# Two output projections with the low activation beside the high one in 512-column matmuls, and both halves of the bank added by VectorE

## What is computed

```python
def even_layer(h, w_in, conv_w, conv_b, gx_w, gx_b, ga_w, ga_b, lru_lambda, sinks, w_out):
    ...
    return jnp.concatenate([y_a, y_b], axis=-1) @ w_out

def odd_layer(h, w_in, q_norm, w_uq, kv_norm, w_ukv, lambda_q1, lambda_k1, lambda_q2, lambda_k2,
              subln, w_out):
    ...
    return jnp.concatenate([y_c, y_d], axis=-1) @ w_out

def second_block(...):
    for layer in range(DEPTH_2):
        h = rmsnorm_2(x, norm_gains[layer])
        if layer % 2 == 0:
            x = x + even_layer(h, *even_params)
        else:
            x = x + odd_layer(h, *odd_params)
    return rmsnorm_2(x, final_norm_gain)
```

## Time and profile before

| | |
|---|---|
| median of 3 runs | 2313.37 us (2312.64 to 2315.13) |
| the profiled execution's own time | 2312.69 us |
| its span | 2310.9 us |
| granted TensorE clock, mean | 0.987 of full |
| TensorE matmul busy | 2070.4 us, 90% |
| VectorE busy | 1248.6 us, 54% |
| ScalarE busy | 868.1 us, 38% |

### The profile page before, as it was taken

How to read it: one execution, slowest core, us unless ns; L and a number is a source line. 1 busy time by engine, 2 the same in 40 slices (tenths; PEclk the granted TensorE clock), 3 DMA queues, 4 the chain that set the end, 5 groups by cost and what they waited for, 6 DMA issues and landing times.

```text
span 2310.9 us, 38449 instructions
## 1 busy us (share of the span) xinstructions
PE 2070.4 (90%) x14546; PEld 1350.6 (58%) x14546; DVE 1248.6 (54%) x2271; ACT 868.1 (38%) x1329; POOL 55.0 (2%) x56
## 2 busy tenths in 40 slices
PE   6899998998988888888888888899999999999998
PEld 2677767772222222222222222799899999998898
DVE  3455567545444444444444444677766554468655
ACT  3343344431211111111111111567756544466654
POOL 0000000000000000000000000110100000011000
PEclk9999999999999999999999999899999999999999
DMA  9998876889999999999999999554445555543443
GB/s 373 366 350 302 311 285 243 293 337 404 427 427 428 427 428 427 428 427 427 428 428 427 427 427 427 198 175 147 141 146 183 176 177 185 178 157 119 142 126 112
DMA packets 121943, 695.42 MB, mean 301 GB/s; under 512 B 13536, under 2 KB 13664, under 8 KB 60384
## 3 DMA queue, kind: packets, MB, share of 16 engines
q1 hardware_dynamic: 121824, 693.78, 77.8%
HBM read 691.63 MB, written 2.10 MB: 300 GB/s over the span
## 4 chain that ended last, share of the span: by engine, by line
PE 45%; DMA 34%; DVE 10%; ACT 5%; SPq 3%; issue 3%; DVEq 0%; ACTq 0%
DMA ring<-in_w 30%; PE acc L1289 29%; DVE WL L2045 3%; PE psO L1348 3%; DMA land<-in_stream_a 3%; PE psS L1557 3%; PE acc L1286 3%; ACT WH L1726 2%; SPq L1103 2%; DMA land<-in_stream_bc 1%; PE acc L1156 1%; PE psM L1156 1%; PE psO L1228 1%; DVE HL L2058 1%; DVE X L2200 1%
## 5 line engine op out<-in xcount | busy, mean ns | idle before, releaser
L2045 DVE TENSOR_TENSOR WL<-land,WH 128x1024 fp32r<-128x1024 f32 (+2 forms) x346 | 416.9, 1206 | 396.1 <-ACT WH L1726 391.8
L1289 PE MATMUL acc<-HH,WH 128*128 128x256 f32 x2000 | 586.2, 293 | 4.2 <-DVE HL L2064 2.2
L1289 PE MATMUL acc<-HH,WL 128*128 128x256 f32 x2000 | 568.9, 284 | 0.0
L1289 PE MATMUL acc<-HL,WH 128*128 128x256 f32 x2000 | 568.5, 284 | 0.0
L1726 ACT ACTIVATE WH<-land 128x1024 fp32r<-128x1024 f32 (+2 forms) x350 | 362.5, 1037 | 207.7 <-PE acc L1289 151.8
L1289 PEld LDWEIGHTS acc<-HH,WH 128*128 128x128 f32 x2000 | 386.8, 193 | 26.5 <-issue 12.6
L1289 PEld LDWEIGHTS acc<-HH,WL 128*128 128x128 f32 x2000 | 387.1, 194 | 2.6 <-issue 2.0
L1289 PEld LDWEIGHTS acc<-HL,WH 128*128 128x128 f32 x2000 | 386.5, 193 | 0.0
L1557 PE MATMUL psS<-ring,low 128*32 128x512 f32 x2048 | 272.6, 604 | 102.3 <-DMA ring<-in_w 100.6
L1557 PEld LDWEIGHTS psS<-ring,low 128*32 128x32 f32 x2048 | 40.7, 108 | 312.7 <-DMA ring<-in_w 284.8
L1887 ACT ACT_TABLE_LOAD x32 | 41.1, 1283 | 442.1 <-PE psS L1557 442.1
(11 more groups left out here) (425 smaller groups left out, 2611.7 us busy)
## 6 DMA issues: line engine op xcount, KB each, us to landing
ring<-in_w SPq DMA_DIRECT2D x384, 1024.0 KB, 26.0
land<-in_stream_bc SPq DMA_DIRECT2D x246, 512.0 KB, 4.1
land<-in_stream_a SPq DMA_DIRECT2D x92, 1024.0 KB, 8.0
land<-in_stream_a SPq DMA_DIRECT2D x100, 512.0 KB, 6.6
land<-in_stream_bc SPq DMA_DIRECT2D x12, 384.0 KB, 3.7
X<-in_xT SPq DMA_DIRECT2D x1, 2048.0 KB, 15.7
out<-low SPq DMA_DIRECT2D x3, 512.0 KB, 2.7
cst<-in_const SPq DMA_DIRECT2D x1, 1514.5 KB, 10.4
```

What stands on the lines that cost most here:

```text
L1289: mm = pe.matmul(bank[:, 0:S], w[:, kk, :], h[rows[kk]], start=(z == 0 and i == 0), stop=stop)
L2045: ins = dve.tensor_tensor(wl, src, wh, ALU.subtract)
```

## The change

In `wb` and `wc` alone, the operands HH and HL of one block are now read as one operand of 2 x 256 columns, so that WH by HH and WH by HL become one matmul of 512 columns, into both halves of the bank. In each weight half eight of these come first; they wait only for `hi`. Then TensorE waits for `lo`, and eight matmuls of 256 columns, WL by HH, go to the first half of the bank. ScalarE's `evac` n and VectorE's `res` n go; a VectorE step `evac` n takes the place of `res` n and adds first one half of the bank to X and then, after a wait for that, the other.

```diff
 def evac_by(x):
-    return "dve" if x[0] in ("bk", "p") or x == LAST_OUT else "act"
+    return "dve" if x[0] in ("bk", "p", "wb", "wc") else "act"
...
         if post == "res":
-            if x != LAST_OUT:
+            if x[0] not in ("wb", "wc"):
                 self.add("dve", "res", x)
...
+        def mix_pair(k, name, c):
+
+            if name == "wb":
+                hi, lo = MIX_HI[c // 4] + c % 4, MIX_LO[c // 4] + c % 4
+                return lowR[:, min(hi, lo):max(hi, lo) + 1:abs(hi - lo), :]
+            return HXs[k][:, :, c, :]
...
-                needs(k, o.lo_by[q], o, "lo", q)
+                if name in ("wb", "wc"):
+                    needs(k, "act", o, "hi", q)
+                else:
+                    needs(k, o.lo_by[q], o, "lo", q)
...
+                if name in ("wb", "wc"):
+                    for kk in range(len(rows)):
+                        if n == 0 and kk % 4 == 0:
+                            needs(k, "dve", o, "ml", name, rows[kk] // 4)
+                        pe.matmul(bank[:, :].rearrange("p (z s) -> p z s", z=2), wh[:, kk, :], mix_pair(k, name, rows[kk]),
+                                  start=(i == 0 and kk == 0), stop=False, skip_group_check=True)
+                    needs(k, o.lo_by[q], o, "lo", q)
+                    for kk in range(len(rows)):
+                        mm = pe.matmul(bank[:, 0:S], wl[:, kk, :], HH[rows[kk]], start=False,
+                                       stop=(last and kk == len(rows) - 1), skip_group_check=True)
+                    mm.then_inc(done[k]["pe"], 1)
+                    return
...
                     elif what == "sq":
                         x = step[1]
                         n = x[1]
-                        needs("dve", "evac" if x == LAST_OUT else "res", x)
+                        needs("dve", "evac" if x[0] in ("wb", "wc") else "res", x)
...
-                        if name == "wc":
+                        if name in ("wb", "wc"):
+                            then(dve.tensor_tensor(X[:, n, :], X[:, n, :], bank[:, S:2 * S], ALU.add))
                             ins = dve.tensor_tensor(X[:, n, :], X[:, n, :], bank[:, 0:S], ALU.add)
```

More of the change, by code:

```diff
@@ L876, in program @@
         WLs = [inside(f"WL{k}", [P, PARTS, HALF], F32R, parts_at[k] + 4 * PARTS) for k in range(2)]
-        HHs = [inside(f"HH{k}", [P, KD, S], F32R, parts_at[k] + 8 * PARTS) for k in range(2)]
-        HLs = [inside(f"HL{k}", [P, KD, S], F32R, parts_at[k] + 8 * PARTS + KD) for k in range(2)]
+        HXs = [inside(f"HX{k}", [P, 2, KD, S], F32R, parts_at[k] + 8 * PARTS) for k in range(2)]
+        HHs, HLs = ([h[:, z, :, :] for h in HXs] for z in range(2))
         land = [inside(f"land{k}", [P, LAND[k], HALF], F32, 0) for k in range(2)]
@@ L938, in program @@
         cDQ, cDK = 16, 24
-        dRT, dT2, dTM, dSQ, dSA, dKX = 58, 59, 60, 62, 64, 66
+        dRT, dT2, dSQ, dSA, dKX = 58, 59, 62, 64, 66
         dV, dRQ, dVE = 51, 52, 53
@@ L1280, in product @@
                             needs(k, "dve", o, "cl", *(("cq", kk) if name == "qr" else ("ckv", kk)))
-                        if x in (("wp", 0), ("wo", 0), ("wb", 0), ("wc", 0)) and term == 0 and kk % 4 == 0:
-                            needs(k, "dve", o, "ml", "wo" if name == "wp" else name, rows[kk] // 4)
+                        if x in (("wp", 0), ("wo", 0)) and term == 0 and kk % 4 == 0:
+                            needs(k, "dve", o, "ml", "wo", rows[kk] // 4)
                         stop = last and z == len(terms) - 1
@@ L1656, in evac @@
                         return act.activation(W(MIX + 8 + c)[:, 0, :], a, ACT.Copy, scale=C("pool_scale", c, 1))
-                    if name in ("wp", "wo", "wb", "wc"):
+                    if name in ("wp", "wo"):
                         if n >= 2:
@@ L1663, in evac @@
                             needs("dve", "res", ("wp", n + KD - 2))
[L1664 to L1667, removed]
+                        return act.activation(W(aTM + n % 2)[:, 0, :], a, ACT.Copy, scale=gt1[:, n:n + 1])
                     if name == "h2t":
@@ L1736, in run @@
                         else:
-                            needs("dve", "res", (name, 4 * (c // 8) + c % 4 if name == "moe" else c))
+                            needs("dve", *(("evac", (name, c)) if name == "wb" else ("res", (name, 4 * (c // 8) + c % 4))))
                             if name == "wb" and c == 0:
@@ L1810, in run @@
                         n = step[1]
-                        needs("dve", *(("evac", LAST_OUT) if n == KD - 1 else ("res", ("wc", n))))
+                        needs("dve", "evac", ("wc", n))
                         ins = act.activation(W(MIX + n)[:, 0, :], X[:, n, :], ACT.Copy, scale=C("gain_f", n, 1))
@@ L2198, in run @@
                             needs("act", "evac", step[1])
-                            tm = W((aTM if k == 0 else dTM) + n % 2)[:, 0, :]
+                            tm = W(aTM + n % 2)[:, 0, :]
                             ins = dve.tensor_tensor(X[:, n, :], X[:, n, :], tm, ALU.add)
@@ L2240, in run @@
                         needs("pe", "proj", x)
-                        bank = acc[o.acc.index(("proj", x)) % 2]
+                        bank = (*bankS, psM[:, :])[SPARE[x]] if x in SPARE else acc[o.acc.index(("proj", x)) % 2]
                         if name == "p":
```

## The result

The changed kernel takes 2320.87 us (median of 7 runs, 2320.4 to 2324.1). The kernel before, run beside it, takes 2313.37 (7 runs, 2310.13 to 2317.59). The ratio is 1.0037, 95% interval [1.0026, 1.0048]: slower by 7.5 us, where 10.4 were predicted, and 0.9 above the lower end of the predicted range.

The account below looks back on a forecast made before the run. It took a closed VectorE-ScalarE loop (5.62 us a turn), tied with TensorE (5.70), as the bound. Terms -1.0 + 0.6 + 0 + 6.4 + 4.4 = +10.4 us took 2312.69 to 2323.1, as median 2323.8; range 2320 to 2327.

Parts of the forecast that it names:

- The second add in the loop: VectorE's second add lengthens each turn of the closed VectorE-ScalarE loop by 0.46 us, from 5.62 to 6.08; +6.4 in `wb`.
- The count of 14: Turns of the loop in `wb` from chunk 1 to chunk 15, each charged 0.46 us for the second add.
- The sum for `wc`: In `wc` 14 longer turns make 6.4, but part falls into the loop's lag: +4.4, besides the order and head terms.
- the tail: End of `wc`: ScalarE's table load and squares after chunk 14's adds delay TensorE's `ss` from 2298.89 to 2303.25; +4.4.
- the order: First second half of each stage: more matmul time remains after the wait for the mix's second part; +0.6 for both stages.
- five heads: First halves at the head of `wc`, where TensorE is on the chain; each gains 0.11 us from wide matmuls.
- It will wait some tenths per projection, hidden by the loop: TensorE waits for its bank, now freed only after VectorE's two adds; this was to cost nothing.
- in wc down to the end: Sign: the chain that ended last runs through VectorE and ScalarE in both stages, in `wc` until its end.
- TensorE's gain: A wide matmul takes 0.227 us, a half 2.78 for 2.89; it counts only in nine first halves at stage heads: -1.0.
- ScalarE's copy: ScalarE's 0.39 us evac stands outside the loop; removing it saves about 0.5 per stage, against one add more: together 0.
- TensorE as the bound: Rival: TensorE sets the pace in all 64 halves, 64 x -0.11 = -7, about 2306.5 us; chance 0.06.
- The clock rival: TensorE's clock falls after a wait of about 1.5 us before HL of chunk 15: +1.4, 2325.2 us; chance 0.10.

Follow-up runs that it names:

- e3: Changed kernel with each 512-column matmul split into two of 256 columns, both adds kept: 2325.08 us, ratio 1.0066 to the kernel before.
- e1: Changed kernel without VectorE's first add, wide matmuls kept: 2308.04 us, ratio 0.9989 to the kernel before.
- e11: Changed kernel with one VectorE add issued twice, so three adds: 2339.75 us, ratio 1.0107 to the kernel before.
- e4: Changed kernel with its two adds one place earlier in VectorE's list, ahead of the second WL: 2308.65 us, ratio 0.9991 to the kernel before.
- e6: Changed kernel with ScalarE's `hi` (WH of the next half) ahead of its squares in `wb` and `wc`: 2305.46 us, ratio 0.9966 to the kernel before.
- e9: Changed kernel run again, nothing edited: 2322.22 us, ratio 1.0033 to the kernel before.
- e10: Kernel before run again, nothing edited: 2312.58 us, ratio 0.9995.
- e2: Kernel before with its 24 narrow matmuls per half, but no ScalarE copy and one VectorE add straight from the bank: 2311.17 us, ratio 0.9998.
- e5: Kernel before with ScalarE's copy of the bank and VectorE's add one place earlier in their lists: 2309.72 us, ratio 0.9986.
- e7: Kernel before with ScalarE's `hi` ahead of its squares in `wb` and `wc`: 2311.03 us, ratio 0.9986.
- e8: Changed kernel with both reorderings, WH ahead of the squares and adds ahead of the second WL: 2304.32 us, ratio 0.9959 to the kernel before.

## Why the prediction was right, and where it was off

Sign, mechanism and range held: 2320.87, in 2320 to 2327, but close to its lower end. By its own steps, profiled span against span (+7.7, predicted +10.4):

*The second add in the loop, +6.4 in `wb`: right.* The turn went from 5.62 to 6.06 (6.08 predicted), the adds start 0.45 to 0.46 apart, and with heads and order the stage grew by 6.65 where these terms made 6.3. e3 shows the loss without wide matmuls, e1 its absence without the add, e11 the same price for one more. That it comes from the closed loop, and not from VectorE's load, is shown by e4 and e6, which keep both adds and lose nothing. The count of 14 is a little low: e1 to e3 put the second add at 7.7 in `wb`, and e11 one more at 7.4, which is 16 adds of 0.46. The prediction had set one more add per stage against the copy that goes, and called the two even; by the 6.65 in `wb` they nearly are.

*The sum for `wc`: right in size, by another way in its last step.* The terms made +4.4 for the tail, +0.3 for the order and -0.55 for five heads, about 4.2. With a fall of the clock at the head in both kernels (e9 against e10) it is 4.7, 4.3 without the slow `ss` of e9. But "TensorE's `ss`" was to be held by ScalarE's table load and squares. In fact the bank held it: the step "It will wait some tenths per projection, hidden by the loop" fails for the last projection, where no loop is left to hide it, and TensorE starts it only behind the adds of chunk 13. So the sign "in wc down to the end" did not come: the chain ends with TensorE's 5.88 us. The two ways end within some tenths of each other, so the number survived.

*What was missing is luck of one execution.* In `wc` the clock did not fall at the head of the changed kernel's profiled execution, though the wait ahead was the same 2.20 us: -1.4. The stretch ahead of `wb` was 2.0 shorter, which e9 and e10 show to be no effect of the change (e10 is 3.4 shorter than the first execution of the very same program). With 0.35 more in `wb` and 0.3 in `wc`: 10.4 - 1.4 - 2.0 + 0.65 = 7.7. In the medians the difference is 7.5 once and 9.4 the other time (the ratios, 1.0037 and 1.0033, come to 8.6 and 7.6). The forecast lacked a term for it: that of the clock at the heads, which can come or stay away in either kernel.

*TensorE's gain, -1.0: right.* A wide matmul takes 0.23 (0.227 taken), a half 2.80 (2.78), so nine heads give 0.8. The Trainium skill (TensorE: Matmul & The Clock Gate, Back-to-back issue gap) has about 131 ns for 512 columns in such a stream; no run here came near it, and its figure for an isolated one, 216 ns, is the nearer of the two.

*ScalarE's copy, 0: right.* e2 is the kernel before without it, 0.9998.

*The rivals.* TensorE as the bound is refuted by the changed kernel and becomes true in e6, once the loop is open; there the wide matmuls give the 0.2% that they can. The rule in the Trainium skill (Perfetto Trace Analysis, Identifying the Most-Contended Engine), which would have had me relieve TensorE first, fails here for that reason: an engine with weight loads at 0.995 of a stage was tied with a chain that never touched it, and relieving the one by adding to the other lost. The clock rival came true in a form that cost nothing. In the middle of `wc` TensorE now waits 1.79 us and its clock falls:

```profile
2245.00:2250.00 5.00, 3.48 (x11) 2.90 (x12) 3.38 (x5) 2.41 (x3) 0.00 (x0) 0.73 0.38 133
```

But the chain there is with VectorE and ScalarE, and their turn stays near 6.1 (the adds at 2243.37, 2249.46 and 2255.55). Ahead of `cq`, the place that the prediction named, it did not fall in the changed kernel; in e11 it did, and cost 1.5 us, near the 1.4 that the rival had as its price.

What stays open: whether the falls at the heads come in equal shares of the executions in both kernels. Two profiled executions of each don't say. Nor do the runs show why a wait is followed by a fall in one execution and not in another.

## What to carry to other kernels

When a busy engine and a closed chain of other engines need the same time per turn (here 5.70 and 5.62 us), relieving the engine is worth next to nothing until the chain is opened (in `wb` e1 is no shorter than e2, in `wc`, where TensorE was slower than the loop, it is 2.1 shorter); look at the chain of waits before the shares, and add up what stands in its loop. An instruction put into such a loop costs its full issue-to-issue time in every turn, however idle its engine is (VectorE was at 54%), and the same instruction is free once one step of the list is moved: ScalarE's split ahead of its squares turned a loss of 0.37% into a gain of 0.34%. And take the stages of a trace, not its span, for anything under 3 us where a long part lies ahead that the change does not touch.

## What the hardware showed that I had not expected

The granted clock after a wait is not settled by the wait. TensorE waited 2.20 us for the same instruction at the head of `wc` in all four profiled executions of the two kernels; in three the clock fell to 1.2 GHz, in one it stayed at 2.4. With the edited kernels there are 13 profiled executions with this wait, of 2.20 or 2.21 us each: the clock fell in 8 (before, e3, e4, e5, e7, e8, e9, e10) and stayed in 5 (after, e1, e2, e6, e11). A fall costs about 1.4 us if TensorE is on the chain then (1.4 between the two executions of the changed kernel, 1.5 ahead of `cq` in e11), and nothing if not (2245 to 2250 above, after a wait of 1.79).

VectorE's add of 128x256 float32 took 0.42 us from the bank and from the temporary alike; two adds one after the other to the same tile start 0.45 to 0.46 apart.
